# Residual sums, norm and transposes taken tile by tile at the layer boundaries of a two-layer hybrid decoder step on one Trainium2 core

## What is computed

```
for l in range(2):
    h = h + concat(HGRN2 heads, differential attention heads) @ w_o
    h = h + hier_moe(rms_norm(h, ffn_norm_w[l]))
y = rms_norm(h, final_norm_w)
```

## Time and profile before

| | us |
|---|---|
| median of 3 runs | 2099.64 (2099.26 to 2105.79) |
| the profiled execution, its own time | 2101.31 |
| its span in the trace | 2099.6 |
| PE busy | 1868.8, 89% of the span |
| PE with nothing to do between the layers | 999.5 to 1026.2 |
| first projection group of the second layer | starts at 1036.63 |
| last sums done, at the end | 2079.62 |
| final norm weight there | 2082.94 |
| last DVE instruction ends | 2090.54 |

### The profile page before, as it was taken

One profiled execution on the slowest core, in us unless ns is written; L12 is line 12 of the kernel. 1 busy time (PEld: TensorE's weight loads), 2 busy tenths in 40 slices (PEclk: granted clock), 3 DMA queues, 4 the chain that ended last, 5 costly groups with the idle time before them and its releaser, 6 DMA issues. The chain is left out here.

```text
span 2099.6 us, 30189 instructions
## 1 busy us (share of the span) xinstructions
PE 1868.8 (89%) x11372; PEld 1095.0 (52%) x11372; DVE 595.4 (28%) x1635; ACT 505.8 (24%) x1072; POOL 183.3 (9%) x236
## 2 busy tenths in 40 slices
PE   7999978887979999999499998888898899999970
PEld 3467755664454454444245776566444444554430
DVE  3205445332242111110420453534313311111103
ACT  2123245644010011111111233565411011111001
POOL 1000012101000001000200000210100010010002
PEclk9999989998979999999799999999998899999985
DMA  8311068986534988986612103988862389988744
GB/s 287 124 68 50 1 205 300 320 294 236 221 123 155 329 307 317 332 327 216 244 56 107 41 21 117 329 295 300 299 234 103 110 317 330 329 299 327 269 150 147
DMA packets 209281, 453.23 MB, mean 216 GB/s; under 512 B 23217, under 2 KB 23218, under 8 KB 209138
## 3 DMA queue, kind: packets, MB, share of 16 engines
q1 hardware_dynamic: 189986, 383.52, 52.4%
q0 software_dynamic: 19152, 67.77, 8.4%
HBM read 413.89 MB, written 37.36 MB: 215 GB/s over the span
## 5 line engine op out<-in xcount | busy, mean ns | idle before, releaser
L910 PE MATMUL bank<-wslots,heads 128*128 128x512 f32 x768 | 339.0, 598 | 2.8 <-DVE heads L1623 2.8
L621 PE MATMUL bank<-xT,wslots 128*128 128x272 f32 x1024 | 241.8, 393 | 1.5 <-ACT heads L1170 0.8
L910 PEld LDWEIGHTS bank<-wslots,heads 128*128 128x128 f32 x768 | 146.3, 192 | 182.0 <-issue 178.4
L621 PEld LDWEIGHTS bank<-xT,wslots 128*128 128x128 f32 x1024 | 191.8, 190 | 40.5 <-issue 3.2
L662 PE MATMUL bank<-cst,wslots 128*128 128x128 f32 x1024 | 164.6, 289 | 17.7 <-ACT wslots L1220 7.2
L575 PE MATMUL bank<-wslots,xT 128*128 128x512 f32 x384 | 172.2, 604 | 0.0
L1753 DVE SCALAR_TENSOR_TENSOR temps<-temps,smalls,bank 128x512 f32<-128x512 f32 x32 | 23.9, 747 | 432.7 <-PE bank L910 432.7
L662 PEld LDWEIGHTS bank<-cst,wslots 128*128 128x128 f32 x1024 | 116.0, 145 | 47.1 <-issue 37.3
L575 PEld LDWEIGHTS bank<-wslots,xT 128*128 128x128 f32 x384 | 72.5, 193 | 89.3 <-issue 89.1
L862 PE MATMUL bank<-wslots,xT 128*128 128x512 f32 x256 | 115.1, 610 | 3.8 <-DVE xT L1522 3.8
L931 PE MATMUL bank<-wslots,temps 128*128 128x512 f32 x256 | 112.7, 593 | 1.5 <-ACT temps L1262 1.5
(11 more groups left out here) (332 smaller groups left out, 2077.9 us busy)
## 6 DMA issues: line engine op xcount, KB each, us to landing
wslots<-in_w_up SPq DMA_DIRECT2D x33, 2048.0 KB, 21.2
wslots<-in_cache_k SPq DMA_DIRECT2D x256, 256.0 KB, 4.5
wslots<-in_cache_v SPq DMA_DIRECT2D x256, 256.0 KB, 4.6
wslots<-in_w_gate SPq DMA_DIRECT2D x17, 2048.0 KB, 16.3
hgrn<-in_w_down SPq DMA_DIRECT2D x17, 2048.0 KB, 10.6
hgrn<-in_w_gate SPq DMA_DIRECT2D x16, 2048.0 KB, 16.5
wslots<-in_w_down SPq DMA_DIRECT2D x16, 2048.0 KB, 10.6
wslots<-in_w_in SPq DMA_DIRECT2D x14, 2048.0 KB, 10.0
```

The costliest lines, as they stand in the source:

```text
L621: x = mm(bank[6 + g % 2][:, 0:HALF], w[:, c, h * P:(h + 1) * P], xT[:, c, half * HALF:(half + 1) * HALF], start=(c == 0), stop=(c == DC - 1))
L910: x = mm(bank[2 + k][:, :], xeT[e % 2][:, c, :], w[:, c, :], start=(c == 0), stop=(c == DC - 1))
```

## The change

The final sums become a function `combined(l, i)` for one tile. In the norm of a later layer and in the final norm, DVE does tile 0's sums, then for each tile first the sums of the next tile and then the norm steps of this one. The sample tile's gathered rows move from the `xn` buffers to free space beside the others. PE's list has the transposes of tile 0 first, and those of tile `n + 1` ahead of projection step `n`; `sample_parts(l, 0)` follows the transposes of tile 4. `turn_qk(n)` now follows `proj_tok(n + 4)`. ACT's two exponentials of the first layer come after its second copy. SP loads the final norm weight as soon as the second layer's router logits are done (in its list it stands behind the extra tiles), and DVE waits for it only after the first tile's `norm_tile`.

```diff
-        yg = [h_a[:, 1024 * i:1024 * (i + 1)] for i in range(8)] + [m_a[:, 0:1024], m_a[:, 1024:2048]]
+        yg = [h_a[:, 1024 * i:1024 * (i + 1)] for i in range(2 * NT)]
...
-                sp.wait_ge(moe_add, 10 * L)
+                sp.wait_ge(lg_ps, NT * L)
                 sp.dma_start(xT_a[:, 0:D], t_in["final_norm_w"].rearrange("(o n) -> o n", o=1).to_broadcast([P, D])).then_inc(first, 16)
...
-                if i == PT - 1:
+                if i == PT - 1 and s:
                     sample_parts(l, s)
...
-                for i in range(NT):
-                    norm_turn(2 * l, i)
+                norm_turn(2 * l, 0)
                 for n in range(15):
+                    if n < NT - 1:
+                        norm_turn(2 * l, n + 1)
+                    if n == PT - 1:
+                        sample_parts(l, 0)
                     proj_tok(l, n)
-                    if 1 <= n <= 10:
-                        turn_qk(l, n - 1)
+                    if 4 <= n <= 13:
+                        turn_qk(l, n - 4)
...
                 norm_roots(2 * l)
-                if l == 0:
-
-                    act.wait_ge(prep_v, 1)
-                    A(lbe[:, :, :], lbe[:, :, :], ACT.Exp).then_inc(prep_a, 1)
-                    A(dls[:, :, :], dls[:, :, :], ACT.Exp).then_inc(prep_a, 1)
                 for n in range(15):
+                    if l == 0 and n == 2:
+
+                        act.wait_ge(prep_v, 1)
+                        A(lbe[:, :, :], lbe[:, :, :], ACT.Exp).then_inc(prep_a, 1)
+                        A(dls[:, :, :], dls[:, :, :], ACT.Exp).then_inc(prep_a, 1)
...
+            def combined(l, i):
+
+                r = rows(i)
+                dve.wait_ge(yg_in[i], 32 * (l + 1))
+                for k in range(2):
+                    link(V.tensor_tensor(hid[0:r, i, :], hid[0:r, i, :], yg[2 * i + k][0:r, :], ALU.add), moe_add)
+
             def norm(m):
+                if m:
+                    combined(m // 2 - 1, 0)
                 for i in range(NT):
+                    if m and i + 1 < NT:
+                        combined(m // 2 - 1, i + 1)
                     norm_tile(m, i)
                     if i >= 1:
                         norm_out(m, i - 1)
...
-                for i in range(NT):
-                    r = rows(i)
-                    dve.wait_ge(yg_in[i], 32 * (l + 1))
-                    for k in range(2):
-                        link(V.tensor_tensor(hid[0:r, i, :], hid[0:r, i, :], yg[2 * i + k][0:r, :], ALU.add), moe_add)
-            dve.wait_ge(first, 48)
+            combined(L - 1, 0)
             for i in range(NT):
+                if i + 1 < NT:
+                    combined(L - 1, i + 1)
                 r = rows(i)
                 norm_tile(2 * L, i)
+                if i == 0:
+                    dve.wait_ge(first, 48)
                 link(V.scalar_tensor_tensor(hid[0:r, i, :], hid[0:r, i, :], rs[0:r, i:i + 1], xT_a[0:r, 0:D], ALU.mult, ALU.mult), out_ok)
```

## The result

The changed kernel takes 2088.35 us (median of 5 runs, 2086.72 to 2092.92), the kernel before in the same sessions 2100.9 (5 runs, 2099.26 to 2105.79). The ratio is 0.9946, with a 95% interval of 0.993 to 0.9963: **0.54% faster**, 12.5 us by the medians, where 9.3 were forecast. The profiled execution took 2086.72 us, with a span of 2085.0 against 2099.6.

What follows compares the result with a forecast made beforehand. PE, busy 89% of the span, was taken as the bound, so only its waits could be won. Second layer's start 6.7 plus end 4.2 less first layer 1.6 gives 9.3 us: 2099.6 to 2090.3 us, range 2085.0 to 2096.0.

Steps and rivals of the forecast that it cites:

- First group 13.1 us earlier: Between the layers: PE's first projection group starts near 1023.5 instead of 1036.63, 13.1 us earlier.
- Transposes and tile 4's wait 3.0 us: Between the layers: transposes now between projection groups, plus the wait for tile 4's placing, add 3.0 us.
- The clock 1.6 us: Second layer's group 0: begins at half speed until the clock rises, losing 1.6 us (bounds 0.8 to 3.5).
- Rival A: Early groups run cold: clock rise counts from group 0, losing 2.95 us instead of 1.6; 2091.6 us; chance 0.12.
- The later turns 1.8 us a layer: PE waits for ACT's copies ahead of group 7 (0.9) and `sample_sum(1)` (1.45); net 1.8 us lost per layer.
- Rival C: Closed loop: turns wait for rotary embeddings, 2.8 us in each of eight groups of both layers; 2130 us; chance 0.04.
- The first layer 1.6 us slower: First layer: group 0 starts 3.2 us earlier, but transposes add 3.0 and turns 1.8; net 1.6 us slower.
- The end 4.2 us: Final sums and norm: early weight load and tile-by-tile order gain 4.2 us (bounds 3.2 and 4.4).
- Rival B: Only the end gains, 4.2 us: cache-page transfers or ACT's roots take back the rest; 2095.4 us; chance 0.14.

Runs made afterwards that it cites:

- Experiments 2 and 3: 2: changed kernel with PE's list and ACT's exponentials as before, 2096.14 us; 3: changed kernel with all sums ahead of the norm between layers, 2092.98 us.
- experiment 8: Changed kernel with turns three steps behind, plus transposes nobody reads where PE waits (40 in the second layer, 30 in the first): 2080.61 us, ratio 0.9894.
- experiment 4: Kernel before with the changed end alone (early final norm weight, sums and final norm tile by tile): 2096.97 us, ratio 0.9978.
- Experiment 1: Changed kernel with turns of queries and keys three steps behind the projection instead of four (the kernel with three steps): 2084.3 us, ratio 0.9937.
- the second pair of profiles: Both kernels unmodified, one more execution each for their stretches: changed kernel 2092.79 us, kernel before 2104.37 us.

## Why the prediction was right, point by point

The forecast of 2090.3 us was 2 us too high, and 2088.35 lies within 2085 to 2096. Each wait that it named stood where it said; some sizes were off. Of its sum:

**First group 13.1 us earlier: right.** It starts 19.34 us after the first gather (1003.29 to 1022.63), before 32.47: 13.1. Experiments 2 and 3 show what it hangs on: sums alone bring 1.3 us, PE's order alone 5.9 of earlier start, and of that 1.4 reach the features. Together it is 8.4 us at the features, because only then has PE both a tile to work on and leave to do it.

**Transposes and tile 4's wait 3.0 us: right.** 0.87 + 0.87 + 1.20 = 2.9, with 0.53 of wait where 0.5 was taken.

**The clock 1.6 us: the term that was mis-sized most between the layers.** The changed kernel lost 0.6 and 0.5 us (groups of 7.61 and 7.54 against 7.03), the kernel with three steps 2.2; the bounds of 0.8 to 3.5 had 0.6 outside. The weak step was to make a fixed delay of three rises at other places. One of them was also misread: the rise 3.2 us into a stretch of the earlier trace rows that begins at 1536.80, while the matmuls in it begin at 1537.19, 2.8 us before the rise:

```profile
1537.19 9.38 PE L862 MATMUL bank<-wslots,xT 128*128 128x512 f32 x18 [1.90 <-DVE xT L1522]
```

With 2.8 the lower bound would have been 0.6, what was measured. No fixed delay fits all the traces: with the same work in the same order, the rise came 1.2 us after the start of the first group in the changed kernel (1.0 in its second execution) and 4.3 us after it with three steps. How much the changed kernel lost to the clock is thus in part chance. Rival A falls for this kernel. By the rule of the Trainium skill that I had set beside it (TensorE: Matmul & The Clock Gate, Part 4: PE-mode transpose: transposes do not count as PE work in the same way) the transposes of experiment 8 should not have raised the clock, and in the second layer they did; the measurement decides. But experiment 4 has the other side, in two stretches between its layers, all transposes and then the first 4 us of matmuls:

```profile
1020.30:1031.00 10.70, 8.93 (x40) 7.20 (x41) 9.46 (x17) 0.45 (x3) 0.00 (x0) 0.50 1.05 387
1031.00:1035.00 4.00, 4.00 (x6) 1.85 (x6) 0.29 (x1) 0.00 (x0) 0.00 (x0) 0.50 0.44 159
```

There the clock stayed at 0.50 through 10.7 us of transposes with waits between tiles, and through 4 us of matmuls; the earlier trace rows had it at 0.50 for 8.7 us of the same and then 1.00. Back to back they raised it in 2.9 us; with gaps they did or did not, and what decides is not shown.

**The later turns 1.8 us a layer: right in place, a little large.** 0.83 and 1.22 us, less the two waits of 0.27 that went, is 1.5. Experiment 1 takes the cause away and both go: it is the fourth step, with ACT's copy of one group behind a turn that PE does one group later. Rival C falls: no wait for a rotary embedding is seen.

**The first layer 1.6 us slower: right in sign and size** (1.1 in this pair of profiles), with two terms off that cancel by luck. The first weight block let PE start at 19.86, not 18.8; and the first group lost 2.0 us (28.71 less 19.86 less 6.9), not 2.9. The pair isn't the whole of it either: the features start at 121.6 to 123.1 in the five executions with PE's list as before, and at 124.1 to 124.4 in the three with the changed list, 1.9 us by the means. That the 2.0 us are the clock is shown by the spacing of the weight loads (last section): it halves at 23.7 us, where the trace's first clock record stands. In experiment 8, at full pace, the same group took 7.13 us.

**The end 4.2 us: right, a little small** (4.54, above the bound of 4.4, and 4.6 by the time of experiment 4; 5.4 by the second pair of profiles); 3.4 the weight, 1.2 the order. The stores did not follow at the same distance: the 0.3 us less behind the last multiply were not in the forecast.

**Rival B falls:** the medians keep the whole gain (12.5 us), not the end's 4.5 alone, and PE waits for no copy ahead of group 2. In sum, by the first pair of profiles, the forecast missed 2.6 us in the three changed stretches (9.3 against 11.9): 1.7 between the layers (1.0 of clock, 0.3 of waits for ACT, 0.1 of transposes, 0.3 unexplained), 0.3 at the end and 0.5 in the first layer.

## What to carry to other kernels

Where a stage waits for a chain of sums, norm and transposes, tile-by-tile order must be given to every engine in the chain: here each half alone was worth 0 to 1.4 us at the next stage, both together 8.4. When a step is moved back in one engine's list, count who holds a buffer until it is done: one step too many cost 2 us a layer, and three steps did the same work without a wait. Where PE must wait anyway, work that nobody reads can be worth its place: with 30 to 40 transposes per layer the first group behind the wait took 2.0 to 2.2 us less than where it began at 1.2 GHz, and the time was 3.7 us lower by the medians. (The groups are those of one execution; where the changed kernel lost only 0.6 us to the clock, in its second layer, there is less to win.)

## What the runs showed of the hardware

PEclk reads 1.00 where a trace has no clock record, so a 1.00 ahead of the first record says nothing. In the first layer of the changed kernel the weight loads of group 0 stand 0.85 us apart up to 23.44 us and 0.43 us from 23.99, with PEclk printed as 1.00 in all of it; but the first clock record of this trace stands at 23.68, of 1.00 from there.

```profile
21.73 0.34 PEld L575 LDWEIGHTS bank<-wslots,xT 128*128 128x128 f32 x1 [0.52 <-issue]
22.58 0.34 PEld L575 LDWEIGHTS bank<-wslots,xT 128*128 128x128 f32 x1 [0.52 <-issue]
23.44 0.31 PEld L575 LDWEIGHTS bank<-wslots,xT 128*128 128x128 f32 x1 [0.52 <-issue]
23.99 0.19 PEld L575 LDWEIGHTS bank<-wslots,xT 128*128 128x128 f32 x1 [0.24 <-issue]
24.42 0.19 PEld L575 LDWEIGHTS bank<-wslots,xT 128*128 128x128 f32 x1 [0.24 <-issue]
24.85 0.19 PEld L575 LDWEIGHTS bank<-wslots,xT 128*128 128x128 f32 x1 [0.24 <-issue]
```

The spacing of 0.85 us is that of the lower level: in experiment 1, second layer, where PEclk reads 0.50 up to 1020.9, the weight loads of the same group stand as far apart.

```profile
1017.39 0.34 PEld L575 LDWEIGHTS bank<-wslots,xT 128*128 128x128 f32 x1 [0.52 <-issue]
1018.24 0.34 PEld L575 LDWEIGHTS bank<-wslots,xT 128*128 128x128 f32 x1 [0.52 <-issue]
```

So where PEclk and the weight loads seem to differ, go by the weight loads.

The other surprise is the spread of a stage with the same instructions: 398.9 to 405.2 us for the attention stretch, more than most terms of this change. A gain of 2 us here is read from a stretch between two events, not from the time of the whole. What makes the attention vary was not tried.
